# Turning softmax probabilities with a diagonal of reciprocals, in a two-block transformer kernel

## The chip, the cores and the metric

One NeuronCore of one Trainium2 chip. The metric is the device time of one execution in microseconds (us), the median of several executions. TensorE is called PE in the profile, its weight loads PEld, VectorE is DVE, ScalarE is ACT, GpSimd is POOL and the queue that issues the transfers is SP.

## The reference

Two blocks of two layers each, on one sequence of 256 tokens and 1024 features, in float32. Three of the stages are attention with a softmax, and these are all that the change touches:

```python
# "mla": 8 heads, query/key 128+64 wide, value 128
p = jax.nn.softmax(sc, axis=-1); o = jnp.einsum('bhqk,bkhd->bqhd', p, v)
# "even": 8 heads with a forget decay (fox), then 8 heads over a shared latent (dsa) with a top-64 choice
p = jax.nn.softmax(s, axis=-1);  ... p = jax.nn.softmax(logits, axis=-1)
# "moba": 16 heads of 64, causal (the 256 tokens are one block of keys)
p = jax.nn.softmax(s_own, axis=-1)
```

Around them stand a conformer convolution, squared-ReLU and gated feed-forward layers, and normalizations. Their matrix products take most of the time.

## The kernel before

All activations lie with features on the partitions and the 256 tokens along the free axis. Weights stream from memory in units of 128 x 4096 float32 values. ACT makes the high float16 part of each half unit (`w_hi`, line 1358), DVE the low part (`w_lo`, line 1992), and a product of float32 quality is three float16 products (lines 618 to 620, also 629 to 631, 1236 to 1238, 1294 to 1296), each 128 x 128 weights against 256 columns. Every engine runs a list of instructions written out by hand, and semaphores join them. Each engine takes its own list strictly in order.

The softmax works with queries on the partitions. A head's scores are two spans beside each other, the first 128 queries against 128 keys and the second 128 queries against 256 keys: 384 columns (`SPAN`). The steps of a head `hd`, with the semaphores of the table `A` in brackets:

- PE multiplies queries and keys in float32 into PSUM (line 786 in "mla" and "even", line 1261 in "moba") [`scores`].
- DVE scales, masks and takes the row maximum (lines 2132 and 2569), then negates it into `peak[2:4]` (lines 2136 and 2572) [`peak`].
- ACT writes `probs = exp(score - max)` and the row sums into `peak[4:6]` (lines 1458 and 1845) [`exp`].
- DVE writes the reciprocals of the two sums into `peak[6:8]` (lines 2144 and 2579) [`inv`].
- POOL multiplies the rows of `probs` by them, in place, one instruction for each span (`divide`, line 1914, and `divide_pair`, line 1960) [`norm`].
- PE turns the three 128 x 128 blocks of `probs` into PSUM with `pe.transpose` against the constant `ident` (lines 797 and 1272) [`turn`]. In these instructions `probs` is the stationary operand and `ident` the moving one.
- ACT copies the turned block to `probsT` (lines 1467 and 1854) [`probsT`]. PE multiplies the values by it (lines 819, 820 and 1283) [`out`]. ACT and DVE split the output into two float16 parts (`x_hi` line 1481 and `x_lo` line 2147, `f_hi` line 1834 and `f_lo` line 2584) [`o_hi`, `o_lo`].

In "mla" and "even" the function `attention` runs on each engine, one step `i` for each head. In step `i` PE makes the scores of head `i`, turns head `i - 3` (`TURN_LAG`) and multiplies the values of head `i - 4` (`OUT_LAG`). In "mla" a slice of the following product `wo` runs between heads (line 629). In step `i` DVE reduces head `i`, inverts the sums of head `i - 1`, makes one `x_lo` and splits a quarter of a weight half (line 2116). The buffers are `probs` three deep, and `peak`, `scores` and `probsT` two deep.

In "moba" the heads go in eight pairs, woven into the projections of the following pair. PE's loop, and around it DVE's:

```python
for p in range(last_pair):              # PE
    pair_product(p + 1, 0, 0, DC // 2); swap_pair(p)
    pair_product(p + 1, 0, DC // 2, DC); pair_product(p + 1, 1, 0, DC // 2)
    score_pair(p)
    if p: turn_pair(p - 1)
    pair_product(p + 1, 1, DC // 2, DC)
    if p: out_pair(p - 1)
# DVE: invert_pair(p - 1), low_pair(p - 2), rope_pair(p), weight splits, reduce_pair(p)
```

`rope_pair` (lines 2556 and 2559) needs `swap_pair` of PE (line 1248) and POOL's `cosine` (line 1950), and `score_pair` needs `rope_pair`. After the loop PE begins the output product `outo` (`behind_pairs`, line 1294), first waiting for ACT to have evacuated the last projection (line 1814). ACT does that behind the exponentials of pair 6.

## Time and profile before

| | us |
|---|---|
| median of 3 runs | 1237.71 |
| lowest and highest of them | 1233.33, 1250.34 |
| the profiled execution | 1241.19 |
| its span, from first to last instruction | 1239.4 |

The page of the profile gives the busy time of each engine, the chain of work that ended last, and groups of instructions. Besides it, the trace can be asked for the instructions of one engine in order of time, for who waited for whom, and for the busy time of each engine in chosen stretches. The attention stages lie at about 359 to 400 us ("mla"), 671 to 734 us ("even") and 949 to 1036 us ("moba"). A float32 product appears as two instructions, each with its own weight load. A turning with `pe.transpose` appears as one.

### The profile page before, as it was taken

The numbers are of one execution on the slowest core, as the hardware profiler recorded it, in microseconds if no ns is written. First come the engines' busy times: TensorE is split into PE (matmuls) and PEld (weight loads), VectorE is DVE, ScalarE is ACT, GpSimd is POOL, SyncE is SP. The second block draws the span as 40 slices with busy tenths as digits, with TensorE's granted clock in tenths as the row PEclk, the third lists the DMA queues.
The fourth block names the chain that finished last, engine by engine and source line by source line (L and its number), as shares of the span: only waits on it lengthen the run. The fifth ranks groups of instructions, "written<-read, shape, count | busy, mean of one in ns | idle before, by whom it ended". The sixth has DMA issues, their size and how long they took to land.

```text
span 1239.4 us, 26482 instructions
## 1 busy us (share of the span) xinstructions
PE 1190.2 (96%) x10692; PEld 998.2 (81%) x10692; DVE 831.9 (67%) x1352; ACT 661.3 (53%) x1046; POOL 128.2 (10%) x160
## 2 busy tenths in 40 slices
PE   8999999999989999999989999999999987999997
PEld 6778888888757888888875668888887766888886
DVE  6766786655954886655695447877666654887764
ACT  6564566433655566433453656665446654765432
POOL 0000100000122100000211421000123531000000
PEclk9998999999998999999999999999999999999998
DMA  7650365555341355555361033654565332555451
GB/s 318 244 200 24 108 233 203 204 203 203 104 169 68 136 204 203 204 203 203 115 226 69 8 129 136 216 199 163 182 233 196 136 137 77 201 205 197 149 196 63
DMA packets 17932, 206.58 MB, mean 167 GB/s; under 512 B 1984, under 2 KB 3392, under 8 KB 5056
## 3 DMA queue, kind: packets, MB, share of 16 engines
q1 hardware_dynamic: 17856, 205.52, 45.7%
q8 instruction: 54, 0.88, 0.3%
q14 instruction: 22, 0.18, 0.0%
HBM read 204.46 MB, written 1.05 MB: 166 GB/s over the span
## 4 chain that ended last, share of the span: by engine, by line
PE 82%; DVE 10%; ACT 4%; DMA 2%; issue 2%; POOL 0%; SPq 0%; DVEq 0%; ACTq 0%
PE ps L618 20%; PE ps L620 20%; PE ps L619 20%; PE ps L786 4%; DVE w_lo L1992 3%; DMA staged<-weights 2%; PE ps L884 2%; ACT w_hi L1358 1%; DVE stat L2006 1%; PE ps L819 1%; PE ps L629 1%; PE ps L1236 1%; PE ps L734 1%; PE ps L631 1%; PE ps L1237 1%
## 5 line engine op out<-in xcount | busy, mean ns | idle before, releaser
L1358 ACT ACTIVATE w_hi<-staged 128x2048 f16<-128x2048 f32 (+3 forms) x191 | 337.3, 1783 | 247.7 <-PE ps L620 212.9
L618 PE MATMUL ps<-f_hi,w_hi 128*128 128x256 f16 x1628 | 444.9, 273 | 8.3 <-DVE h L2086 7.1
L619 PE MATMUL ps<-f_lo,w_hi 128*128 128x256 f16 x1628 | 444.9, 273 | 0.0
L620 PE MATMUL ps<-f_hi,w_lo 128*128 128x256 f16 x1628 | 444.9, 273 | 0.0
L1992 DVE SCALAR_TENSOR_TENSOR w_lo<-staged,w_hi 128x2048 f16<-128x2048 f32 (+3 forms) x191 | 407.4, 2148 | 40.0 <-ACT w_hi L1358 39.8
L618 PE MATMUL ps<-x_hi,w_hi 128*128 128x256 f16 x880 | 240.1, 273 | 0.7 <-DVE tmp L2282 0.6
L620 PE MATMUL ps<-x_hi,w_lo 128*128 128x256 f16 x880 | 239.9, 273 | 0.0
L619 PE MATMUL ps<-x_lo,w_hi 128*128 128x256 f16 x880 | 239.9, 273 | 0.0
L618 PEld LDWEIGHTS ps<-f_hi,w_hi 128*128 128x128 f16 x1628 | 159.7, 98 | 28.5 <-DVE h L2086 7.4
L619 PEld LDWEIGHTS ps<-f_lo,w_hi 128*128 128x128 f16 x1628 | 159.7, 98 | 19.5
L620 PEld LDWEIGHTS ps<-f_hi,w_lo 128*128 128x128 f16 x1628 | 159.7, 98 | 18.9
L618 PEld LDWEIGHTS ps<-x_hi,w_hi 128*128 128x128 f16 x880 | 86.1, 98 | 17.6 <-issue 5.0
L619 PEld LDWEIGHTS ps<-x_lo,w_hi 128*128 128x128 f16 x880 | 86.1, 98 | 11.0
L620 PEld LDWEIGHTS ps<-x_hi,w_lo 128*128 128x128 f16 x880 | 86.1, 98 | 10.0
L1922 POOL TENSOR_TENSOR h<-h,m 128x256 f32<-128x256 f32 x28 | 23.9, 882 | 503.6 <-DVE m L2039 503.6
L2308 DVE TENSOR_SCALAR m<-ps 128x256 f32 (+1 forms) x16 | 6.8, 424 | 63.4 <-PE ps L620 54.4
L1761 ACT ACTIVATE tmp<-pad,vec 128x256 f32<-128x256 f32 x44 | 26.4, 599 | 42.1 <-DVE pad L2473 37.9
L2282 DVE SCALAR_TENSOR_TENSOR tmp<-ps,stat 128x256 f32<-128x256 f32 x64 | 26.8, 419 | 26.2 <-PE ps L620 26.1
L2473 DVE TENSOR_TENSOR pad<-ps,stat 128x256 f32<-128x256 f32 x44 | 18.6, 423 | 31.6 <-PE ps L620 31.6
L1458 ACT ACTIVATE probs<-scores,peak 128x128 f32<-128x128 f32 (+1 forms) x48 | 21.4, 446 | 28.9 <-DVE peak L2136 28.9
L1592 ACT ACTIVATE tmp<-tmp 128x256 f32<-128x256 f32 x64 | 26.2, 409 | 17.4 <-DVE tmp L2282 17.4
L1914 POOL TENSOR_TENSOR probs<-probs,peak 128x128 f32<-128x128 f32 (+1 forms) x48 | 28.5, 615 | 64.9 <-DVE peak L2144 64.9
(312 smaller groups left out, 1680.8 us busy)
## 6 DMA issues: line engine op xcount, KB each, us to landing
staged<-weights SPq DMA_DIRECT2D x82, 2048.0 KB, 8.0
staged<-weights SPq DMA_DIRECT2D x16, 1408.0 KB, 6.1
xn<-bands SPq DMA_DIRECT2D x3, 512.0 KB, 9.6
m<-bands SPq DMA_DIRECT2D x3, 512.0 KB, 8.4
cst<-constants SPq DMA_DIRECT2D x1, 1029.0 KB, 10.5
h<-x_turned SPq DMA_DIRECT2D x2, 512.0 KB, 5.0
staged<-weights SPq DMA_DIRECT2D x2, 512.0 KB, 7.0
staged<-weights SPq DMA_DIRECT2D x1, 1024.0 KB, 9.2
```

The lines of the kernel that those rows point to most:

```text
L618: pe.matmul(out, wh, xh[:, c, :], start=(c == 0), stop=False)
L619: pe.matmul(out, wh, xl[:, c, :], start=False, stop=False)
L620: last = pe.matmul(out, wl, xh[:, c, :], start=False, stop=(c == kc - 1))
L786: last = pe.matmul(o[:, P * t:P * t + P * (t + 1)], a, b, start=(n == 0), stop=(n == len(terms) - 1))
L884: last = pe.matmul(ps[BAND * g:BAND * g + BAND, 3, 0:T], banded[w][:, (j * TAP_SET + g) * TAP_STEPS + step, :], shifted[:, j % 2, x, g, TA ...
L1358: act.activation(w_hi[:, s, o:o + n], staged[:, s, o:o + n], ACT.Copy, scale=SW).then_inc(hi_split, 1)
L1592: act.activation(tmp[:, 2 + n % 2:3 + n % 2, :], r, ACT.Square)
L1761: act.activation(tmp[:, j, :], pad[:, j, 0:T], ACT.Identity, bias=vec[:, bass.ds(i * 4 + (VCOL[f"b_cv_{layer}"] + n), 1)], scale=vec[:, ba ...
L1914: last = pool.tensor_tensor(probs[:, hd % 3, sl], probs[:, hd % 3, sl], peak[:, hd % 2, 6 + t:7 + t].to_broadcast([P, P * (t + 1)]), ALU.mult)
L1922: pool.tensor_tensor(h[:, c, :], h[:, c, :], m[:, c, :], ALU.add).then_inc(h_ready[ready], 1)
L1992: dve.scalar_tensor_tensor(w_lo[:, s, o:o + n], staged[:, s, o:o + n], SW, w_hi[:, s, o:o + n], ALU.mult, ALU.subtract).then_inc(lo_split, 1)
L2282: dve.scalar_tensor_tensor(tmp[:, n % 2, :], ps[:, n % RING, 0:T], 0.0, LATE_SCALE, ALU.max, ALU.mult).then_inc(drained[one], 1)
```

## The change

GpSimd's `divide` and `divide_pair` are gone. After its reciprocal, VectorE waits for that reciprocal to be written, makes two 128 x 128 diagonals for the head (`ident` times the reciprocal of each row) in a new buffer `shares_diag`, and raises `norm` itself. TensorE turns with an ordinary float32 product: `probs` stays the stationary operand, the moving operand is the diagonal in place of `ident`, and so the turned block comes out scaled. VectorE's wait ahead of the reciprocal is now for the turning of the head (or pair) that used the buffer before, where it was for GpSimd's scaling.

```diff
+        shares_diag = sb("shares_diag", [P, 2, TT, P])
@@ tensor, attention
                         for n in range(3):
-                            last = pe.transpose(o[:, P * n:P * n + P], probs[:, hd % 3, P * n:P * n + P], k("ident"))
+                            last = pe.matmul(o[:, P * n:P * n + P], probs[:, hd % 3, P * n:P * n + P],
+                                             shares_diag[:, hd % 2, min(n, 1), :], start=True, stop=True)
@@ tensor, turn_pair
-                        last = pe.transpose(ps[:, 6 + r, P * n:P * n + P], probs[:, (2 * p + r) % 3, P * n:P * n + P], k("ident"))
+                        last = pe.matmul(ps[:, 6 + r, P * n:P * n + P], probs[:, (2 * p + r) % 3, P * n:P * n + P],
+                                         shares_diag[:, r, min(n, 1), :], start=True, stop=True)
@@ gpsimd
-            def divide(kind):
-                at = before(kind)
-                for hd in range(KINDS[kind]["heads"]):
-                    pool.wait_ge(A["inv"], at["inv"] + hd + 1)
-                    for t in range(TT):
-                        sl = slice(P * t, P * t + P * (t + 1))
-                        last = pool.tensor_tensor(probs[:, hd % 3, sl], probs[:, hd % 3, sl],
-                                                  peak[:, hd % 2, 6 + t:7 + t].to_broadcast([P, P * (t + 1)]), ALU.mult)
-                    last.then_inc(A["norm"], 1)
-            divide("mla")
-            divide("even")
-            def divide_pair(p):
-                ...
-                if p:
-                    divide_pair(p - 1)
-            divide_pair(last_pair)
@@ vector, attention
-                            dve.wait_ge(A["norm"], at["norm"] + hd - 1)
+                            dve.wait_ge(A["turn"], at["turn"] + hd - 1)
                         dve.reciprocal(peak[:, b, 6:8], peak[:, b, 4:6]).then_inc(A["inv"], 1)
+                        dve.wait_ge(A["inv"], at["inv"] + hd + 1)
+                        for t in range(TT):
+                            last = dve.tensor_scalar(shares_diag[:, b, t, :], k("ident"), peak[:, b, 6 + t:7 + t], None, ALU.mult)
+                        last.then_inc(A["norm"], 1)
@@ vector, invert_pair
-                    dve.wait_ge(A["norm"], heads["norm"] + p)
+                    dve.wait_ge(A["turn"], heads["turn"] + p)
                 dve.reciprocal(peak[:, :, 6:8], peak[:, :, 4:6]).then_inc(A["inv"], 1)
+                dve.wait_ge(A["inv"], heads["inv"] + p + 1)
+                for r in range(2):
+                    for t in range(TT):
+                        last = dve.tensor_scalar(shares_diag[:, r, t, :], k("ident"), peak[:, r, 6 + t:7 + t], None, ALU.mult)
+                last.then_inc(A["norm"], 1)
```

## Rows read from the trace of the kernel before

**Rows 1.** Page, part 1: busy us (share of the span) and instructions of each engine.

```profile
PE 1190.2 (96%) x10692; PEld 998.2 (81%) x10692; DVE 831.9 (67%) x1352; ACT 661.3 (53%) x1046; POOL 128.2 (10%) x160
```

**Rows 2.** Page, part 4: the chain that ended last, by engine.

```profile
PE 82%; DVE 10%; ACT 4%; DMA 2%; issue 2%; POOL 0%; SPq 0%; DVEq 0%; ACTq 0%
```

**Rows 3.** Busy us of each engine by stretch, then PEclk, DMA share, GB/s.

```profile
367.00:382.00 15.00, 14.28 (x38) 8.65 (x38) 2.82 (x19) 7.33 (x25) 3.88 (x8) 0.56 0.00 1
672.00:716.00 44.00, 42.52 (x203) 26.42 (x201) 18.59 (x92) 25.82 (x81) 16.46 (x26) 1.00 0.09 29
948.00:1014.60 66.60, 66.17 (x525) 48.82 (x522) 44.42 (x94) 39.83 (x84) 33.02 (x37) 1.00 0.38 132
1014.60:1018.00 3.40, 0.16 (x3) 0.14 (x2) 1.85 (x12) 2.37 (x11) 0.17 (x1) 0.89 0.93 390
1018.00:1036.00 18.00, 17.55 (x143) 14.06 (x143) 5.96 (x16) 5.57 (x13) 4.31 (x9) 0.93 0.39 142
```

**Rows 4.** Timeline of PE, a dsa head: start us, us, engine line op tiles.

```profile
700.27 0.49 PE L786 MATMUL ps<-kT,m 128*128 128x128 f32 x2
700.69 0.49 PE L786 MATMUL ps<-qT 64*128 64x128 f32 x2
...
702.36 0.55 PE L797 MATMUL ps<-cst,probs 128*128 128x128 f32 x3
702.84 0.65 PE L819 MATMUL ps<-probsT,f_lo 128*64 128x256 f32 x2
```

**Rows 5.** Timeline of PE, a pair of "moba".

```profile
966.57 0.88 PE L1272 MATMUL ps<-cst,probs 128*128 128x128 f32 x6
967.28 0.27 PE L1236 MATMUL ps<-x_hi,w_hi 128*128 128x256 f16 x1
```

**Rows 6.** Timeline of PE, line 696: two float32 products, broadcast column against `ident`.

```profile
130.43 0.61 PE L696 MATMUL ps<-cst,by_token 128*128 128x128 f32 x4
130.87 1.03 PE L734 MATMUL ps<-decay_k 128*128 128x256 f32 x4
```

**Rows 7.** Timeline of PE, "mla" at the low clock.

```profile
367.72 6.86 PE L786 MATMUL ps<-kT,qT 128*128 128x128 f32 x16 [2.06 <-ACT qT L1428]
...
374.51 0.90 PE L797 MATMUL ps<-cst,probs 128*128 128x128 f32 x3
375.20 3.66 PE L786 MATMUL ps<-kT,qT 128*128 128x128 f32 x8
```

**Rows 8.** Timeline of PE: its idle times behind a turning [idle before <-releaser].

```profile
393.60 0.67 PE L819 MATMUL ps<-probsT,f_lo 128*128 128x256 f32 x2 [1.28 <-DVE x_lo L2147]
...
716.96 0.67 PE L819 MATMUL ps<-probsT,ckvt 128*128 128x256 f32 x2 [0.95 <-DVE x_lo L2147]
...
726.24 0.67 PE L819 MATMUL ps<-probsT,ckvt 128*128 128x256 f32 x2 [0.50 <-ACT tmp L1475]
...
1017.85 0.37 PE L1294 MATMUL ps<-f_hi,w_hi 128*128 128x256 f16 x1 [3.24 <-issue]
```

**Rows 9.** Timeline of DVE, "even", the step in which head 9 is turned.

```profile
715.58 0.29 DVE L2132 CUSTOM_DVE_ANT_0 scores<-ps,sel 128x128 f32<-128x128 f32 x1 [1.51 <-PE ps L786]
...
716.33 0.17 DVE L2144 RECIPROCAL peak<-peak 128x2 f32<-128x2 f32 x1
716.41 0.40 DVE L2147 SCALAR_TENSOR_TENSOR x_lo<-ps,x_hi 128x256 f16<-128x256 f32 x1
```

**Rows 10.** Timeline of DVE, "moba": an undisturbed rope, then around the rope of pair 6.

```profile
1000.31 0.69 DVE L2559 TENSOR_TENSOR qT<-qT,tmp 128x512 f32<-128x512 f32 x1
...
1006.45 0.18 DVE L2579 RECIPROCAL peak<-peak 128x4 f32<-128x4 f32 x1 [1.75 <-ACT probs L1845]
1006.99 0.42 DVE L2584 SCALAR_TENSOR_TENSOR f_lo<-ps,f_hi 128x256 f16<-128x256 f32 x1 [0.36 <-ACT f_hi L1834]
1008.26 0.69 DVE L2556 TENSOR_TENSOR tmp<-ps,tmp 128x512 f32<-128x512 f32 x1 [0.84 <-PE ps L1248]
1008.98 0.91 DVE L2559 TENSOR_TENSOR kT<-kT,tmp 128x512 f32<-128x512 f32 x1
```

**Rows 11.** Timeline of DVE: a 128x128 and a 128x256 scaling by a column.

```profile
635.87 0.54 DVE L2418 TENSOR_SCALAR idx<-scores,gates 128x128 f32<-128x128 f32 x2
```

**Rows 12.** Timeline of POOL, "moba": a cosine and a scaling of a pair.

```profile
1006.77 0.73 POOL L1950 TENSOR_TENSOR kT<-kT,tmp 128x256 f32<-128x256 f32 x1 [2.98 <-ACT kT L1814]
1007.45 1.90 POOL L1960 TENSOR_TENSOR probs<-probs,peak 128x128 f32<-128x128 f32 x4
```

**Rows 13.** Line 797: its idle before, by releaser: us, times.

```profile
L797 PE MATMUL ps<-cst,probs x72: 272/273/473, 374.5 to 729.6; 128*128 128x128 f32 x72
its engine sat idle before it (us, times) until:
  issue: 6.1, 16
```

**Rows 14.** Page, part 5: GpSimd's scaling of single heads: busy, mean ns | idle before.

```profile
L1914 POOL TENSOR_TENSOR probs<-probs,peak 128x128 f32<-128x128 f32 (+1 forms) x48 | 28.5, 615 | 64.9 <-DVE peak L2144 64.9
```

More of the change, by code:

```diff
@@ L1951, in cosine @@
                     normed_rows, 1)
-            def divide_pair(p):
-                pool.wait_ge(A["inv"], heads["inv"] + p + 1)
-                for r in range(2):
-                    for t in range(TT):
-                        sl = slice(P * t, P * t + P * (t + 1))
-                        at = probs[:, (2 * p + r) % 3, sl]
-                        last = pool.tensor_tensor(at, at, peak[:, r, 6 + t:7 + t].to_broadcast([P, P * (t + 1)]), ALU.mult)
-                last.then_inc(A["norm"], 1)
             pool.wait_ge(tables, 2)
```

## The prediction

> **What bounds the kernel now.** I read the page first. TensorE is busy 96% of the span and holds 82% of the chain that ended last, GpSimd is busy 10% and holds none of it [rows 1, 2]. An average over the span says little about three attention stages, so next came the busy time by stretch. In "even" and in "moba" up to its end TensorE is busy 42.52 of 44 us and 66.17 of 66.6 us, at the full granted clock, while VectorE has more than a quarter of each stretch free [rows 3]. There every tenth that TensorE's list grows is a tenth of the end. The exceptions are four idle times that lie behind a turning [rows 8], and a part of "mla" at the low clock (0.56 granted on the mean over 15 us, so about 13.2 of the 15 at half speed) [rows 3].
>
> Then, who waits for the instruction that the change removes. The idle time ahead of the turning, 6.1 us in 16 places, ends on "issue", none of it on GpSimd's `probs` [rows 13]. This label belongs to the weight loads, which are not always back to back. No turning waits for a scaling: scores and turning are three steps apart, and the scaling of a pair takes 1.90 us [rows 12]. So removing GpSimd's 80 instructions takes nothing from the path.
>
> **The change part by part.**
>
> *GpSimd's scaling goes: 0.* What hides it now is the lag of three heads. No work waits behind it in its list that TensorE waits for either: each `cosine` that a pair needs stands ahead of the scaling of the pair before.
>
> *The turning becomes a product: the main term.* A turned block is one instruction today. A float32 product is two. The nearest row is line 696, float32, 128 x 128 stationary against 128 columns of `ident`, the same form as the new turning: its two products are four instructions that start within 0.44 us, 0.11 us each [rows 6]. Turned blocks go at about 0.11 us each as well: six of them and the switch to the next kind take 0.71 us [rows 5], three take 0.48 us [rows 4]. So a head gets three more instructions of 0.11 us, 0.33 us. The first of a group, whose load nothing covers, counts a little more: the second of a float32 product starts 0.49 - 0.27 = 0.22 us behind it, the second of a turning 0.55 - 0.27 - 0.11 = 0.17 us [rows 4], with 0.27 us for the last one's own duration. That adds 0.05. A head costs 0.38 us more, a pair 6 x 0.11 + 0.05 = 0.71 us.
>
> The bounds of this price: not under 0.33 us, since no row has a float32 product of 128 columns in less than two times 0.11 us. At most what line 786 shows, 0.42 us for a product of the same size (700.27 to 700.69) [rows 4]. There the second load is not hidden. I take the low end, because line 786 changes from 128 to 64 rows between products and the new turning, like line 696, doesn't.
>
> - "mla", 8 heads. Heads 0 and 1 are turned at the low clock (0.69 us from 374.51 to 375.20 for three blocks [rows 7]), so they pay double, 0.76 us. Heads 4 and 5 are turned ahead of 1.28 us of idle that ends on `x_lo` of VectorE, which hangs on the scores of head 7 and not on the turning [rows 8]: nothing. 2 x 0.76 + 4 x 0.38 = **3.0 us**.
> - "even", 16 heads: 16 x 0.38 = 6.1 us. Head 9 is turned ahead of 0.95 us of idle, and one idle time of 0.50 us near the end takes up what it can [rows 8]: 6.1 - 0.38 - 0.50 = **5.2 us**, before VectorE's part.
> - "moba", 8 pairs. Pair 5 is turned between the swap of pair 6 and the idle time of 3.24 us, whose end hangs on VectorE's rope, two weight splits and the reduction of pair 6, and then ACT's exponentials [rows 8, 10]: nothing. 7 x 0.71 = **5.0 us**.
>
> *VectorE's diagonals.* 80 new instructions of 128 x 128. The row of two scalings by a column, 128 and 256 wide, takes 0.54 us together [rows 11]. A head's two are at most that, a pair's four 1.08 us; below, 0.2 us each if only the width counts. I take the upper end. Then the wait for the reciprocal's own result, and the wait for the turning two heads back. A new turning of three blocks ends about 0.9 us after the scores, and VectorE reaches its reciprocal 0.75 us after it begins to reduce [rows 9], so that wait costs it some 0.15 us. What is queued behind: the `x_lo` of the step, a quarter split, and the next reduction. The reduction is covered, since VectorE has 1.51 us idle ahead of it [rows 9] against 0.7 us more work. The `x_lo` is covered everywhere but where TensorE waits for it. Head 9 is that place: its `x_lo` starts at 716.41 right behind the reciprocal [rows 9] and comes about 0.15 + 0.54 + 0.06 = **0.75 us** later. In "mla" the `x_lo` at the 1.28 us of idle waits for ACT, and hides the diagonals.
>
> In "moba" VectorE has 0.36 us of idle ahead of `low_pair` and 0.84 us ahead of the rope, 1.20 us together against 1.08 us [rows 10]. Without that cover the rope and the scores behind it would be late. It does hold, by little, so **0**. A rule of the Trainium skill speaks against this. The second SBUF port of VectorE is shared with GpSimd, and instructions that use two ports block each other (Advanced Engine Details and Errata, VectorE Performance Modes, Mode Summary). The trace has a sign of it: the rope's addition takes 0.91 us beside a scaling of GpSimd and 0.69 us where none runs [rows 10, 12]. By that rule the four diagonals would be stretched by the cosine of 0.73 us that runs at the same time, while the rope's addition would get its 0.22 us back, and the sum would be up to 0.4 us higher at pair 6 and unchanged elsewhere. The sum goes by the rows.
>
> **Sum**: 3.0 + 5.2 + 0.75 + 5.0 = 14.0 us. The profiled execution took 1241.2 us and would take 1255.2. It lies 3.5 us above the median of the runs shown, so against the median of 1237.7 I forecast **1252 us**, 1.1% slower. That is within the 2% (24.8 us) which I count as no change, about what a measurement of this kernel can tell.
>
> **The rivals.**
>
> *The loads are not hidden (ends on the other side, slower by over 2%).* Place: the six loads of a turning. Price: 0.42 us a block, as line 786 has it. A head goes from 0.48 to 1.26 us, +0.78, a pair from 0.71 to 2.52 us, +1.81. 24 x 0.78 + 8 x 1.81 = 33.2 us, plus 1.6 for two heads at the low clock, less the idle times that take up some (1.28, 0.50 and pair 5's 1.81): 31 us, so 1269 us. It decides from about 0.32 us a block on: 0.21 us more than today for 120 blocks is 25 us. For it: the two-instruction products of line 786 beside the turning. Against it: rows 6, the very form. 12%.
>
> *The clock stays up.* If TensorE worked at the full clock in "mla" where it has the low one now, 13.2 us of the stretch would take half, 6.6 us back, and the doubled price of two heads falls to the simple one, 0.8 us. The smaller stretch about 1018 us (0.89 over 3.4 us and 0.93 over 18 us, together 3.3 us at half speed [rows 3]) gives back 1.6 us, since the idle ahead of it shrinks from 3.24 to about 2.5 us. 14.0 - 9.0 = 5 us: 1243 us. Against it: the fall in "mla" follows an idle time of 2.06 us ahead of the first turning [rows 7], which no part of the change touches. 12%. The Trainium skill has a rule by which more would come of this: a turning in transpose mode doesn't count as activity for the clock gate (TensorE: Matmul & The Clock Gate, Part 4: PE-mode transpose), and an ordinary product would. By it the low stretch of "mla" would end sooner, for the part of the 6.6 us that is left when head 0 is turned at 374.5. The trace doesn't bear it out: in "even" the clock stays at 1.00 with a turning in every step [rows 3].
>
> *VectorE becomes the bound in "moba".* The cover of 1.20 us fails when the four diagonals run beside a cosine: 1.08 + 0.73 = 1.81 us, 0.6 us over, for 7 pairs 4.3 us, so 1256 us. Against it: the scores of a pair wait a further while for their place in TensorE's list. 10%.
>
> **How the numbers follow.** The forecast has 66%, the three rivals 12, 12 and 10%. The range is 1243 to 1264 us: the clock case at its lower end, the VectorE case inside, and it leaves out the case of unhidden loads and the tails. The three runs of before differ by 17 us, so a few us on either side are the measurement's own. Slower by over 2% is the first rival and a little, 13%. Faster by over 2% would need 25 us that no row offers, 1%. Within 2%: 86%.
>
> **What would show it.** TensorE's instructions grow by 120, to 10812, and nothing on GpSimd waits for `peak` any more. The groups at lines 797 and 1272 show 144 and 96 instructions, a head's six start within about 0.66 us, a pair's twelve within 1.3 us. GpSimd's busy time falls by some 44 us (28.5 in the 24 single heads, 8 x 1.90 = 15 in the pairs) [rows 12, 14], VectorE's grows by about 20 us. The idle time of 0.95 us at head 9 stays about as long, that of 3.24 us shrinks by 0.7 us, and VectorE's idle ahead of the rope nearly vanishes. The prediction is wrong if products in a group start 0.2 us apart, if TensorE waits for VectorE's rope or `norm` in "moba", or if the low clock in "mla" is gone.

## The result

| us, median | before | after |
| --- | --- | --- |
| first chip, 4 runs each | 1238.81 | 1260.41 |
| lowest, highest | 1233.33, 1250.34 | 1258.18, 1261.68 |
| the profiled execution, its span | 1241.19, 1239.4 | 1258.18, 1256.4 |

The ratio of after to before is 1.014, with a 95% interval from 1.009 to 1.020. The quotient of the two medians is 1.017. The kernel is slower, by less than 2%. The forecast was 1252 us in a range from 1243 to 1264. Ratios and intervals in this document leave out the runs that took over 1.5% longer than the fastest of their kernel, medians are of all runs.

The profile after. First the busy time of each engine and the chain that ended last, beside [rows 1, 2]:

```profile
PE 1208.2 (96%) x10812; PEld 1014.3 (81%) x10812; DVE 852.1 (68%) x1432; ACT 661.6 (53%) x1046; POOL 83.4 (7%) x80
...
PE 83%; DVE 9%; ACT 3%; DMA 3%; issue 1%; SPq 0%; POOL 0%; DVEq 0%; ACTq 0%
```

TensorE has 120 instructions more and 18.0 us more of busy time. The span is 17.0 us longer. GpSimd lost 44.8 us of busy time, and the end didn't move towards the start by anything for it: GpSimd held 0% of the chain, and still does. VectorE took on 20.2 us.

The timeline of TensorE around turnings: a head of "even", a pair of "moba" and the pair after it, and a head of "mla" at the low clock. They answer to [rows 4, 5, 7]. Columns are start us, us, engine line operation tiles.

```profile
710.58 0.94 PE L799 MATMUL ps<-shares_diag,probs 128*128 128x128 f32 x6
711.44 0.65 PE L822 MATMUL ps<-probsT,f_lo 128*64 128x256 f32 x2
...
978.98 1.60 PE L1275 MATMUL ps<-shares_diag,probs 128*128 128x128 f32 x12
980.42 0.27 PE L1239 MATMUL ps<-x_hi,w_hi 128*128 128x256 f16 x1
...
988.38 1.60 PE L1275 MATMUL ps<-shares_diag,probs 128*128 128x128 f32 x12
...
375.18 1.65 PE L799 MATMUL ps<-shares_diag,probs 128*128 128x128 f32 x6
376.62 0.63 PE L788 MATMUL ps<-kT,qT 128*128 128x128 f32 x2
```

A head's turning takes 0.86 us up to the next instruction, where it took 0.48. A pair's takes 1.44 us, where it took 0.71. At the low clock a head takes 1.44 us, where it took 0.69. So the three surcharges are 0.38, 0.73 and 0.75 us. Two pairs follow each other at 9.40 us (978.98 to 988.38). Before, the same two stood 8.68 us apart (966.57 to 975.25 by [rows 5] and the row of line 1272 behind it): the surcharge shows in the period, and nothing else in such a step of "moba" grew.

TensorE's idle times behind a turning, beside [rows 8]. The value in brackets is the idle time before the row and what ended it:

```profile
396.74 0.67 PE L822 MATMUL ps<-probsT,f_lo 128*128 128x256 f32 x2 [0.35 <-DVE x_lo L2129]
...
727.44 0.67 PE L822 MATMUL ps<-probsT,ckvt 128*128 128x256 f32 x2 [1.27 <-DVE x_lo L2129]
...
1032.96 0.27 PE L1298 MATMUL ps<-f_hi,w_hi 128*128 128x256 f16 x1 [2.29 <-issue]
```

They were 1.28, 0.95 and 3.24 us. The same three points also measure how far the kernel is behind: 396.74 against 393.60 is 3.1 us at the end of "mla", 727.44 against 716.96 is 10.5 us late in "even", 1032.96 against 1017.85 is 15.1 us near the end of "moba".

The busy time of each engine by stretch, in the columns of [rows 3], for the low clock in "mla", a stretch ahead of "even", and most of "even" and "moba":

```profile
368.30:385.30 17.00, 17.00 (x46) 10.66 (x44) 4.34 (x25) 6.27 (x20) 0.00 (x0) 0.50 0.00 1
651.60:655.00 3.40, 3.40 (x18) 2.35 (x17) 3.37 (x5) 0.00 (x0) 0.00 (x0) 0.50 0.63 265
684.00:727.00 43.00, 40.69 (x201) 27.09 (x198) 24.16 (x112) 26.55 (x84) 0.72 (x1) 1.00 0.12 44
965.00:1030.00 65.00, 64.96 (x510) 49.10 (x512) 46.12 (x106) 36.01 (x73) 17.99 (x12) 1.00 0.36 130
```

"even" and "moba" are bound by TensorE at the full clock, as before. "mla" has the low one for 17 us, and there is a stretch of 3.4 us at the low clock ahead of "even" which the trace of before doesn't have.

**Where the 17.0 us are**, by the distance between the same instructions of the two traces:

| part | us | forecast |
| --- | --- | --- |
| ahead of the first turning | 0.7 | 0 |
| "mla" | 3.15 | 3.0 |
| between "mla" and "even" | 2.3 | 0 |
| "even" | 5.55 | 5.95 |
| "moba" | 5.17 | 5.0 |
| behind it | 0.15 | 0 |

The three stages that turn give 13.9 us, where the working gave 14.0. That they agree so closely is partly luck, as the section on the prediction shows. The other 3 us lie where nothing was changed, and the medians show still more, 21.6 us. That is what was left to explain.

### The profile page after: what moved, and what is told of

It is laid out like the page before. It is cut to its first block, busy times and chain, and to the rows that moved or that the text cites. A ratio compares the mean times of both kernels' runs of the same rounds, so it can differ in the third digit from the quotient of the medians.

```text
span 1256.4 us, 26722 instructions
## 1 busy us (share of the span) xinstructions
PE 1208.2 (96%) x10812; PEld 1014.3 (81%) x10812; DVE 852.1 (68%) x1432; ACT 661.6 (53%) x1046; POOL 83.4 (7%) x80
## 3 DMA queue, kind: packets, MB, share of 16 engines
HBM read 204.46 MB, written 1.05 MB: 164 GB/s over the span
## 4 chain that ended last, share of the span: by engine, by line
PE 83%; DVE 9%; ACT 3%; DMA 3%; issue 1%; SPq 0%; POOL 0%; DVEq 0%; ACTq 0%
PE ps L620 20%; PE ps L621 19%; PE ps L622 19%; PE ps L788 4%; DVE w_lo L1970 3%; DMA staged<-weights 2%; PE ps L887 2%; PE ps L799 2%; ACT w_hi L1362 1%; PE ps L1239 1%; PE ps L822 1%; PE ps L1240 1%; PE ps L1241 1%; DVE stat L1984 1%; PE ps L1275 1%
## 5 line engine op out<-in xcount | busy, mean ns | idle before, releaser
L2256 DVE SCALAR_TENSOR_TENSOR f_lo<-tmp,f_hi 128x256 f32 (+1 forms) x64 | 26.7, 418 | 14.1 <-ACT f_hi L1597 13.6
## 6 DMA issues: line engine op xcount, KB each, us to landing
cst<-constants SPq DMA_DIRECT2D x1, 1029.0 KB, 10.5
```

What stands on the lines that cost most here:

```text
L2256: dve.scalar_tensor_tensor(f_lo[:, at, :], f, SF, f_hi[:, at, :], ALU.mult, ALU.subtract).then_inc(f_lo_ready[layer], 1)
```

## The experiments

The main theory is that of the prediction: the whole loss is TensorE's second instruction for each turned block, the work taken from GpSimd is worth nothing, and VectorE's diagonals are hidden but at one head. The first rival says that VectorE's diagonals cost the time, as they stand ahead of `x_lo` and of the rope. The second says that the granted clock does: that the changed kernel, by its nature, spends another time at the low clock.

Each execution comes with its span and its mean granted clock. The clock has two levels here, full and half, 2.4 and 1.2 GHz, and so the time at the low one is 2 x span x (1 - clock). Over the executions of the kernel before on the chips of the experiments (21, 23 and 33 on the three), the spans lie on 1223.4 us + 0.41 x that time, with a standard deviation of 1.4 us and at most 3.8 us off. So each kernel gets two numbers: the mean time at the low clock, and the **steady part**, its span less 0.41 of that time. The 0.41 is fitted to the kernel before and taken over for the others.

| kernel | runs | median us | ratio to before, 95% | low clock, us | steady part, us |
| --- | --- | --- | --- | --- | --- |
| before (three chips) | 21, 23, 33 | 1243.84, 1243.87, 1244.62 | 1 | 41, 47, 45 | 1223.6, 1223.1, 1223.6 |
| after (first chip) | 4 | 1260.41 | 1.014 [1.009, 1.020] | 54 | 1236.4 |
| after, again | 10 | 1251.36 | 1.0089 [1.0054, 1.0125] | 37 | 1235.2 |
| product alone | 6 | 1257.14 | 1.0136 [1.0085, 1.0187] | 47 | 1235.2 |
| diagonals alone | 6 | 1256.35 | 1.0102 [1.0036, 1.0168] | 74 | 1223.0 |
| VectorE scales | 12 | 1246.94 | 1.0044 [1.0008, 1.0080] | 59 | 1222.9 |
| product twice | 6 | 1277.55 | 1.0263 [1.0205, 1.0321] | 34 | 1260.8 |
| after, `x_lo` first | 6 | 1254.93 | 1.0119 [1.0057, 1.0182] | 47 | 1235.2 |
| VectorE scales, `x_lo` first | 12 | 1243.74 | 1.0009 [0.9967, 1.0051] | 44 | 1223.7 |
| float16 turning | 12 | 1247.25 | 1.0002 [0.9964, 1.0040] | 61 | 1219.0 |
| before, one gap filled | 12 | 1238.49 | 0.9974 [0.9940, 1.0009] | 34 | 1223.1 |
| before, three gaps filled | 12 | 1236.11 | 0.9931 [0.9904, 0.9958] | 21 | 1225.2 |
| after, three gaps filled | 12 | 1247.93 | 1.0035 [1.0008, 1.0062] | 18 | 1238.6 |
| float16 turning, three gaps filled | 10 | 1234.93 | 0.9920 [0.9895, 0.9946] | 31 | 1219.9 |

### The changed kernel again, on another chip

No edit.

> The changed kernel once more. The traces of before and after differ by 13.9 us in the stretches that turn, and by 17.0 us in the span, while the medians differ by 21.6 us. Theory A (the second instruction of each turning product is all of it, the rest is scatter of the runs and low clock elsewhere): 14 to 17 us over before. Rival B (there is a further steady loss that one pair of traces doesn't show): 20 to 23 us over before again.

1251.36 us, a ratio of 1.0089. The loss is 7.5 us by the medians here, against 21.6 us on the first chip. Neither theory had it: 14 to 17 and 20 to 23 us were expected. The steady part is 11.6 us above that of before on the same chip, and was 1236.4 against 1235.2 us for the changed kernel itself. What differs is the time at the low clock: 54 us and 37 us for one and the same program. The busy time by stretch shows it in "mla", here 13.7 us in the columns of [rows 3], in which before and the first trace of after have about half the clock:

```profile
367.50:381.20 13.70, 13.70 (x68) 9.18 (x68) 6.80 (x35) 8.36 (x27) 0.00 (x0) 1.00 0.01 1
```

68 instructions in 13.7 us at the full clock, where the first trace of after had 46 in 17 us. The idle time ahead of "mla" is the same in both, 2.05 and 2.06 us.

### The product alone

GpSimd scales as before, VectorE makes no diagonals. Only the form of the turning changes.

```diff
-last = pe.transpose(o[:, P * n:P * n + P], probs[:, hd % 3, P * n:P * n + P], k("ident"))
+last = pe.matmul(o[:, P * n:P * n + P], probs[:, hd % 3, P * n:P * n + P], k("ident"), start=True, stop=True)
```

The pair's turning has the same edit.

> The kernel before, with the turning as an ordinary float32 product against the constant identity. GpSimd still scales, VectorE makes no diagonals. Theory A (TensorE's instructions are the loss): 13.2 us over before (3.0 in mla, 5.2 in even, 5.0 in moba), a head's group of six instructions 0.38 us longer, a pair's 0.73. Rival C (VectorE's diagonals and its wait for the turning carry a good part): at most 8 us over before.

A steady part of 1235.2 us, the same as that of the changed kernel and 11.6 us above before. The groups are those of after too, here a head of "even", head 9 with the product behind it, and two pairs on TensorE's timeline:

```profile
705.31 0.94 PE L797 MATMUL ps<-cst,probs 128*128 128x128 f32 x6
706.18 0.65 PE L819 MATMUL ps<-probsT,f_lo 128*64 128x256 f32 x2
...
716.22 0.94 PE L797 MATMUL ps<-cst,probs 128*128 128x128 f32 x6
717.72 0.67 PE L819 MATMUL ps<-probsT,ckvt 128*128 128x256 f32 x2 [0.56 <-DVE x_lo L2147]
...
969.25 1.60 PE L1272 MATMUL ps<-cst,probs 128*128 128x128 f32 x12
970.70 0.27 PE L1236 MATMUL ps<-x_hi,w_hi 128*128 128x256 f16 x1
...
978.66 1.60 PE L1272 MATMUL ps<-cst,probs 128*128 128x128 f32 x12
```

0.87 us for a head, 1.45 us for a pair, 9.41 us from pair to pair. With GpSimd's scaling back in place and VectorE's work gone, the whole steady loss is still there. So it is TensorE's, and neither GpSimd's nor VectorE's part of the change moves it by more than such a comparison can tell, about half a us. The rows can tell more: at head 9 the next product starts 1.50 us behind the turning here, just as before (715.47 to 716.96), so the longer turning hides in the idle time, which fell from 0.95 to 0.56 us.

### The diagonals alone

VectorE makes the diagonals and GpSimd is free, but the turning stays `pe.transpose` with `ident`. The division of the softmax is left out.

```diff
-last = pe.matmul(o[:, P * n:P * n + P], probs[:, hd % 3, P * n:P * n + P],
-                 shares_diag[:, hd % 2, min(n, 1), :], start=True, stop=True)
+last = pe.transpose(o[:, P * n:P * n + P], probs[:, hd % 3, P * n:P * n + P], k("ident"))
```

> The changed kernel with the old turning by transpose, so VectorE makes the diagonals and raises the semaphore, and nothing reads them. The probabilities stay unscaled: the softmax division is left out. Theory A: 0.7 us over before, all of it in the wait for x_lo at head 9 (idle 0.95 us grows to 1.6), within the scatter. Rival C (VectorE is what costs): 6 us or more over before. If removing GpSimd's scaling gave something back, it would be under before.

The median, 12.5 us above before, taken alone would have spoken for the rival that blames VectorE. The steady part doesn't: 1223.0 us against 1223.6. All of the difference is time at the low clock, 74 us against 41 on this chip, and 0.41 x 33 = 13.5 us. The trace has the pairs at the period of before (967.16 to 975.84, 8.68 us), and a stretch in "even" at the low clock that neither before nor after shows in theirs. Busy time by stretch, in the columns of [rows 3]:

```profile
719.00:736.00 17.00, 16.69 (x44) 10.54 (x45) 5.47 (x24) 6.41 (x22) 0.00 (x0) 0.50 0.08 32
```

So the diagonals are hidden. That this kernel stayed at the low clock for longer is measured in its six runs, one of which is left out of the ratio. Why is not settled (below).

### VectorE scales the probabilities in place

No diagonals, no product: VectorE does what GpSimd did, 128 and 256 columns by a column, and the turning stays a transposition.

```diff
-last = dve.tensor_scalar(shares_diag[:, b, t, :], k("ident"), peak[:, b, 6 + t:7 + t], None, ALU.mult)
+at_t = probs[:, hd % 3, P * t:P * t + P * (t + 1)]
+last = dve.tensor_scalar(at_t, at_t, peak[:, b, 6 + t:7 + t], None, ALU.mult)
```

> GpSimd's scaling is gone, VectorE scales the probabilities in place with two instructions a head (128 and 256 wide, where the diagonals were 128 and 128), and the turning stays a transpose. The output is the whole one. Theory A: 1 us over before at most, 13 us under the changed kernel, though VectorE does slightly more than for the diagonals. Rival C: no better than the changed kernel.

A steady part of 1222.9 us. This frees GpSimd just as the change does, and costs TensorE nothing that the steady part shows. The ratio of 1.0044 again comes with more time at the low clock, 59 us.

### The product twice

Each product of the turning is issued twice, into the same place and with the same operands. It adds 120 products, 240 instructions.

```diff
+pe.matmul(o[:, P * n:P * n + P], probs[:, hd % 3, P * n:P * n + P], shares_diag[:, hd % 2, min(n, 1), :],
+          start=True, stop=True)
 last = pe.matmul(o[:, P * n:P * n + P], probs[:, hd % 3, P * n:P * n + P],
```

> The changed kernel with every turning product run twice into the same place. Theory A (each further instruction costs TensorE 0.11 us wherever it has no idle time): a head 0.67 us more, a pair 1.34, together 22 to 25 us over the changed kernel, span times granted clock about 1256 (changed kernel 1232, before 1220). Rival (TensorE's list has slack that took part of the change up): under 15 us.

The steady part is 25.6 us above that of the changed kernel, 0.107 us for each added instruction. TensorE's timeline of one pair, which has twelve products of two instructions each. Here are the first four:

```profile
982.62 0.49 PE L1277 MATMUL ps<-shares_diag,probs 128*128 128x128 f32 x2
982.95 0.39 PE L1279 MATMUL ps<-shares_diag,probs 128*128 128x128 f32 x2
983.17 0.39 PE L1277 MATMUL ps<-shares_diag,probs 128*128 128x128 f32 x2
983.39 0.39 PE L1279 MATMUL ps<-shares_diag,probs 128*128 128x128 f32 x2
```

The starts are 0.22 us apart (0.33 for the first), so an instruction with its own weight load costs 0.11 us when another stands ahead of it. The price of line 696 [rows 6] holds in the attention stages, and the end moves by nearly all of TensorE's added time.

### `x_lo` ahead of the diagonals

Does the wait at head 9 cost anything? In VectorE's step the scaling to `x_lo` moves ahead of the reciprocal and the diagonals.

```diff
+for c, b, hd in ended(kind, i - LOW_LAG[kind]):
+    ...
 hd = i - 1
 if 0 <= hd < H:
     ...
-for c, b, hd in ended(kind, i - LOW_LAG[kind]):
-    ...
```

> The changed kernel with VectorE's x_lo ahead of the reciprocal and the diagonals in each step of mla and even. Theory A: the idle time at head 9 falls from 1.27 us to about 0.5, 0.7 us less in span times granted clock, nothing else moves. Rival (the order on VectorE matters elsewhere too): over 2 us either way.

TensorE's idle times that end on `x_lo`, in the timeline of this kernel, "mla" and then head 9:

```profile
388.31 0.67 PE L822 MATMUL ps<-probsT,f_lo 128*128 128x256 f32 x2 [1.00 <-DVE x_lo L2117]
...
718.25 0.67 PE L822 MATMUL ps<-probsT,ckvt 128*128 128x256 f32 x2 [0.49 <-DVE x_lo L2117]
```

The idle time at head 9 goes from 1.27 to 0.49 us, as it should if the diagonals delayed `x_lo`. But one in "mla" is 1.00 us, where the second trace of after has 0.35 us. From the turning to the next product it is 0.77 us less at head 9 (2.20 to 1.43 us) and 0.65 us more at that place of "mla" (1.19 to 1.84). The steady part stays at 1235.2 us, where 0.7 us less was expected. The term at head 9 is real, and this order pays for it in "mla".

The same order in the kernel in which VectorE scales:

> VectorE scales the probabilities in place, the turning is a transpose, and x_lo goes ahead of the reciprocal. Theory D (with transposes an idle time of TensorE in even is what brings the low clock there, and it costs 4 to 10 us): idle at head 9 back at 0.9 us or less, granted clock 0.98 or more as before, and 1 us under before. Rival (the low clock comes with any idle time, whatever is at head 9, since the one ahead of the first turning at 678 us stays at 1.48 us): granted clock 0.967 to 0.982 as without the new order.

1243.74 us, ratio 1.0009, a steady part of 1223.7 us. Its time at the low clock is that of before, 44 us, and its granted clocks run from 0.973 to 0.990 with a median of 0.982. That decides neither way between the two expectations. Theory D isn't borne out by the trace, which has a low stretch in "even" again, at about 677 to 687 us, long before head 9.

### Float16 for the probabilities and the diagonals

Both buffers become float16, so that the product is one instruction again. It rounds the probabilities and the reciprocals. The outputs differ from the float32 ones by 2% and not in the fourth digit, as the expectation has it, so this is a probe and no kernel to keep.

```diff
-probs = sb("probs", [P, 3, SPAN])
+probs = sb("probs", [P, 3, SPAN], F16)
-shares_diag = sb("shares_diag", [P, 2, TT, P])
+shares_diag = sb("shares_diag", [P, 2, TT, P], F16)
```

> The changed kernel with the probabilities and the diagonals in float16, so that a turned block is one float16 instruction in place of two float32 ones. Theory A (the price is the two float32 instructions of a block): the whole 12 us come back, a group of three takes about 0.35 us or less, span less 0.41 times the us at low clock between 1217 and 1224 (before 1223.7, changed 1235.7). Rival C (VectorE and the new waits): it stays above 1230. Rounding to float16 changes the values in the fourth digit.

TensorE's timeline, a head of "even" and two pairs:

```profile
705.48 0.34 PE L799 MATMUL ps<-shares_diag,probs 128*128 128x128 f16 x3
705.75 0.65 PE L822 MATMUL ps<-probsT,f_lo 128*64 128x256 f32 x2
...
968.63 0.51 PE L1275 MATMUL ps<-shares_diag,probs 128*128 128x128 f16 x6
968.98 0.27 PE L1239 MATMUL ps<-x_hi,w_hi 128*128 128x256 f16 x1
...
976.94 0.51 PE L1275 MATMUL ps<-shares_diag,probs 128*128 128x128 f16 x6
```

A head takes 0.27 us and a pair 0.35 us, and the pairs follow at 8.31 us, 0.37 less than before. The steady part is 1219.0 us, 16 to 17 below the changed kernel and 4.6 below before. All other parts of the change are in this kernel. Its median is no better than that of before, since it spent 61 us at the low clock.

### Filled gaps: the clock held still

The long low stretches that the traces have in "mla" and "even" begin behind idle times of TensorE, the one in "mla" behind 2.06 us [rows 7]. The same idle time is followed by the full clock in other traces, as in the second one of after. The kernel has `keep_warm(n)`, products whose result nobody reads, for such places. Here 4 more stand ahead of head 2 of "mla" in the kernel before:

```diff
+keep_warm(4, 7)
 pe.wait_ge(drained["uq"], 12)
 attention("mla", 2, behind="wo")
```

> The kernel before, with eight idle matmuls (four float32 products whose output nobody reads) in TensorE's idle time of 2.06 us ahead of head 2 in mla. Theory D (the idle time brings the low clock of 13.7 us at 368.7 in the trace of before): the stretch is at the full clock, granted clock 0.989 or more in nearly all executions, median 5 to 7 us under before. Rival (the sparse float32 products behind it bring it): granted clock 0.981 as often as before, no gain.

1238.49 us, a ratio of 0.9974, whose interval reaches 1.0009. The mean time at the low clock is 34 us against 47 on this chip. The steady part stays. The gain of 5.4 us by the medians is as large as expected, but not clear of noise.

Then three places: ahead of head 2 of "mla", ahead of head 2 of "even" and, in the second layer, ahead of the gated MLP.

```diff
+keep_warm(3, 7)
 pe.wait_ge(normed_rows, 9)
@@ glu_mlp
+if layer:
+    keep_warm(13, 3)
 pe.wait_ge(h_ready[("oute", "outo")[layer]], (DC - RING + 1, DC - 1)[layer])
```

> The kernel before with idle products in three idle times of TensorE: 4 ahead of head 2 in mla, 3 ahead of head 2 in even, 13 ahead of the last up projection, where it waits 7.14 us. Theory D (each low stretch follows an idle time): at most 23 us at low clock (start, and the last wait), median 8 to 10 us under before, span less 0.41 times low still 1223 to 1224. Rival (sparse products behind them bring it anyway): as with the first of the three alone, 34 us at low clock on the mean.

> The changed kernel with the same three fillings. Theory A: 12 to 13 us over the filled kernel before, and now with little scatter, since both have the same low stretches. Rival B (the change itself adds low clock): 15 us or more over it.

> The float16 turning with the three fillings. Theory A and D together: 8 to 14 us under before, under the filled kernel before by 0 to 6 us.

Before goes to 1236.11 us, 0.7% faster than it was, the fastest of the kernels that compute all that the reference does. The changed kernel with the same edit takes 1247.93 us. Busy time by stretch, of before with three filled gaps and then of the changed kernel with them, "mla" and the MLP behind "moba":

```profile
360.00:400.00 40.00, 38.30 (x236) 28.43 (x235) 19.87 (x71) 23.26 (x62) 8.30 (x16) 1.00 0.19 61
1040.00:1080.00 40.00, 38.30 (x322) 33.54 (x321) 31.99 (x42) 27.22 (x36) 4.53 (x7) 1.00 0.44 159
```

```profile
360.00:400.00 40.00, 39.23 (x243) 29.78 (x244) 22.21 (x84) 22.34 (x61) 0.00 (x0) 1.00 0.15 53
1040.00:1080.00 40.00, 38.31 (x322) 33.27 (x321) 23.01 (x31) 23.11 (x32) 5.20 (x7) 1.00 0.31 112
```

In all four the clock is full. With it nearly the same in both (21 and 18 us low, granted clock 0.991 and 0.992 by the medians), the twelve runs of each lie within 9 and 4 us, and their medians are **11.8 us** apart. The steady parts are 13.4 us apart. This is the cleanest measurement of the change. It hardly leans on the fit for the clock, as 3 us less at the low clock are worth 1.4 us. The float16 turning with the same three fillings takes 1234.93 us, 13.0 us under the changed kernel, though it has 31 us at the low clock against 18. The steady parts are 18.7 us apart. Both come from the float16 turning and what goes with it, since ACT and VectorE now write float16 too.

## Why the prediction was right, and where it was not

*GpSimd's scaling is worth nothing.* Right. The product alone, with the scaling back, has the same steady part as the changed kernel, and VectorE's scaling in GpSimd's place has that of before. GpSimd's busy time fell by 44.8 us, where 44 was announced.

*A product costs one more instruction of 0.11 us, with the load hidden.* Right, and this carried the forecast. 0.38, 0.73 and 0.75 us were measured for a head, a pair and a head at the low clock, where 0.38, 0.71 and 0.76 were written. The two-instruction products of line 786, at 0.42 us for one, are no measure for a group that changes nothing between its products. Doubling the products added 0.107 us an instruction. The 120 added instructions are there, and a group is over in 0.86 and 1.44 us, up to the next instruction, as the announced starts within 0.66 and 1.3 us ask for. The rival with unhidden loads falls: at the full clock no turning has its products 0.42 us apart.

*What the idle times take up.* Nearly right. At the end of "mla" the idle time went from 1.28 to 0.35 us: it took up 0.93, and two heads cost 0.76. Why it is more isn't settled, but the product alone has the same 0.35 us. In "moba" the idle time went from 3.24 to 2.29, 0.95 us where 0.7 was announced. The product alone leaves 2.52 us there, the diagonals alone 3.02. So 0.72 is the turning's and the other 0.22 comes with GpSimd's absence, as much as the rope's addition got shorter (below). The short idle time near the end of "even" took up 0.7 us and not 0.50: the step in which it lies went from 2.45 to 2.11 us from turning to turning, with a turning that is 0.39 us longer.

*VectorE's diagonals at head 9: the term of 0.75 us.* Right in its parts, and nearly in its size. TensorE's timeline of after and VectorE's in that step, beside [rows 9]:

```profile
725.23 0.94 PE L799 MATMUL ps<-shares_diag,probs 128*128 128x128 f32 x6
...
726.02 0.17 DVE L2114 TENSOR_SCALAR peak<-peak 128x2 f32<-128x2 f32 x1
726.28 0.17 DVE L2122 RECIPROCAL peak<-peak 128x2 f32<-128x2 f32 x1
726.48 0.48 DVE L2125 TENSOR_SCALAR shares_diag<-cst,peak 128x128 f32<-128x128 f32 x2
726.87 0.42 DVE L2129 SCALAR_TENSOR_TENSOR x_lo<-ps,x_hi 128x256 f16<-128x256 f32 x1
```

The row ahead of the reciprocal in before, and both rows in the float16 turning, whose turning is over in 0.34 us:

```profile
716.25 0.17 DVE L2136 TENSOR_SCALAR peak<-peak 128x2 f32<-128x2 f32 x1
```

```profile
718.89 0.17 DVE L2114 TENSOR_SCALAR peak<-peak 128x2 f32<-128x2 f32 x1
718.97 0.17 DVE L2122 RECIPROCAL peak<-peak 128x2 f32<-128x2 f32 x1
```

From the negation to the reciprocal it is 0.26 us in after and 0.08 us in both others. So VectorE waits 0.18 us for the turning of two heads back, where 0.15 had been written. Then `x_lo` starts 0.59 us behind the reciprocal, where it started 0.08 us behind it: 0.51 us more, by two diagonals at 0.20 us each from start to start and about 0.1 us of wait for the reciprocal. That had been 0.54 + 0.06 us, with the diagonals priced by a 128 and a 256 wide scaling [rows 11], where the lower bound of 0.2 us each was the true value. Together they make 0.69 us, and TensorE's next product starts 2.20 us behind the turning (725.23 to 727.44) where it started 1.50 us behind it before, and in the product alone. The diagonals alone, whose turning is short, have 2.02 us. So the turning itself costs nothing at this place, and the 0.70 us are VectorE's. One sign contradicted this sum: the idle time was to stay about as long, while 0.95 - 0.38 + 0.75 makes 1.32 us, and it grew to 1.27.

*"mla": 3.15 us against 3.0.* The near agreement is luck in part. The low stretch lasts 17 us in this trace of after and 13.7 in before, by which the step from head 1 to head 2 grew by 1.14 us and not by 0.75. The 0.2 us that the idle time took up beyond the sum stand against it. Between the two kernels with filled gaps, at the full clock on either side, "mla" costs 2.0 us, where six heads at the simple price make 2.3. The doubled price of two heads belongs to the execution and not to the change.

*"even" as a whole: 5.55 us against 5.95.* The price of a head in it was taken from one row of 0.48 us [rows 4]. Not all are alike. TensorE's timeline of before has heads at 0.42 us from the turning to the next instruction:

```profile
695.70 0.49 PE L797 MATMUL ps<-cst,probs 128*128 128x128 f32 x3
696.12 0.65 PE L819 MATMUL ps<-probsT,f_lo 128*64 128x256 f32 x2
```

and that of after has them at 0.76 us:

```profile
699.64 0.83 PE L799 MATMUL ps<-shares_diag,probs 128*128 128x128 f32 x6
700.40 0.65 PE L822 MATMUL ps<-probsT,f_lo 128*64 128x256 f32 x2
```

That is 0.34 us for such a head in place of 0.38. Five heads of "even" have this length, which accounts for 0.2 of the 0.4 us. The idle time near the end accounts for the other 0.2.

*"moba": 5.17 us against 5.0.* Here too two things cancel. The idle time took up 0.22 us more than the turning of a pair costs, and in the step behind it TensorE had some 0.3 us more at the low clock. In before 0.7 us of the low stretch about 1018 us lie in the idle time (0.89 granted over its 3.4 us [rows 3]), in after all of it falls on work (1.00 granted ahead of 1032.96).

*VectorE's cover in "moba": 0.* Right for the time. Here VectorE's timeline at pair 6, beside [rows 10]:

```profile
1021.78 0.18 DVE L2561 RECIPROCAL peak<-peak 128x4 f32<-128x4 f32 x1 [2.48 <-ACT probs L1849]
1022.00 1.35 DVE L2565 TENSOR_SCALAR shares_diag<-cst,peak 128x128 f32<-128x128 f32 x4
1023.26 0.41 DVE L2571 SCALAR_TENSOR_TENSOR f_lo<-ps,f_hi 128x256 f16<-128x256 f32 x1
1023.60 0.68 DVE L2538 TENSOR_TENSOR tmp<-ps,tmp 128x512 f32<-128x512 f32 x1
1024.31 0.69 DVE L2541 TENSOR_TENSOR kT<-kT,tmp 128x512 f32<-128x512 f32 x1
```

And GpSimd's at the same time:

```profile
1022.10 0.77 POOL L1941 TENSOR_TENSOR kT<-kT,tmp 128x256 f32<-128x256 f32 x1 [3.71 <-ACT kT L1818]
```

The four diagonals take 1.35 us beside a cosine of GpSimd, 1.26 up to the next instruction, where four undisturbed ones would take about 0.8 (0.20 each, as at head 9). One of them lasts 0.758 us by line 2565's longest, against a median of 0.278. The rope's addition is back from 0.91 to 0.69 us. VectorE's idle ahead of the rope is gone, as announced, and TensorE still doesn't wait for the rope: the period of the pairs is 9.40 us, all of it explained. No turning in "moba" waits for the diagonals either; near the end of "even" two weight loads are marked with 0.4 us of wait for them, but their steps are no longer than the turning explains (1.70 to 2.09 us). The rival that VectorE becomes the bound had the stretching right and the end wrong. The Trainium skill's rule on the shared SBUF port (Advanced Engine Details and Errata, VectorE Performance Modes, Mode Summary) agrees with this row in its direction, about 0.45 us for the four. The sum didn't grow by it, since TensorE's idle time behind pair 5 became 0.22 us shorter than its longer turning alone makes it.

*The clock.* Here my working was weakest, though the range held. I treated the low stretches of one execution as the kernel's own, and put "the clock stays up" as a mechanism of the changed kernel, with 12%, and the absence of the low clock in "mla" as what would prove me wrong. It is absent in the second trace of after, for reasons that aren't the change's. The runs show a scatter between executions of one program. "mla" has the full clock in the second trace of after, in the product alone and in the version with `x_lo` first, and the low one in the first trace of after, in the product twice, in before and in the diagonals alone. The kernel before was granted from 0.967 to 0.992 over its runs. At 0.41 us for each us at the low clock, that is why its times spread over 17 us on the first chip and over 24 on the second of the others (1232.97 to 1257.11). The first chip's gap of 21.6 us is then made of some 12 us that the change costs and the rest, some 9 us, of the low clock: four executions of after with 54 us of it, and a before whose median, at 1238.81, lies 5 us under that of each later chip. The split rests on the fit, and for before on that chip only the profiled execution has its clock on record, 0.982. That 1260 us lay inside the range, 8 us above the forecast, and 1251 us on the next chip right beside it, was then also a matter of which executions were caught. What doesn't rest on it is the pair with filled gaps, 11.8 us apart. The stretch of 3.4 us ahead of "even", with 1.69 us of idle before it in place of 1.05, is part of the same scatter as far as the traces show; what lengthens that idle time stays open.

*Where the sum stands.* The terms made 14.0 us, and the steady cost is 11.6 to 13.4 by the runs. The turning stages of the two traces gave 13.9, of which about 1.4 us are the low clock's: 0.75 by two heads at the doubled price, 0.4 by the longer low stretch in "mla" and 0.3 in "moba". The mechanism was right, but that the two sums agree to 0.1 us is luck.

*What stays open.* Which executions, and which kernels, get more of the low clock. The Trainium skill has the rule that a turning in transpose mode doesn't count as activity for the clock gate (TensorE: Matmul & The Clock Gate, Part 4: PE-mode transpose). The traces lean its way. Of the six kernels in float32 that turn by transposition, four have a low stretch in "even" (both with a free GpSimd, at 684 to 705 and 719 to 736 us in their traces, VectorE's scaling with `x_lo` first, and before with one gap filled), and none of the six traces in which the turning is a float32 product has one there. Here are two of them, in the columns of [rows 3], before with one gap filled and then the product twice:

```profile
676.00:696.40 20.40, 20.40 (x53) 11.92 (x53) 5.61 (x31) 8.12 (x27) 5.18 (x9) 0.50 0.00 0
```

```profile
672.00:734.00 62.00, 60.52 (x358) 43.56 (x356) 27.86 (x126) 28.27 (x88) 2.90 (x4) 1.00 0.08 27
```

Against it: the float16 turning is an ordinary product as well and has 61 us low, with 0.85 granted over 700 to 745 us, and even with its gaps filled a stretch of 3.4 us in "even"; the first chip's four executions of after have 54 us, more than before; and the low clock in "mla" comes and goes under either form. One trace a kernel doesn't settle it. By the rule the product would give back some of its price in some executions. A gain that the measurement can tell is not among the results: at the same time low, the product costs 11.6 to 13.4 us.

## What to carry to other kernels

Where TensorE is the bound, a float32 product in place of a float32 transposition costs a second instruction (0.11 us a block here), and work taken from an engine that holds none of the chain pays nothing for it; if GpSimd has to be freed, let VectorE do the scaling, in its own free time (1222.9 us steady here, where before has 1223.6). Before a loss or a gain of 1% is put down to an edit, look at the granted clock of every run and compare at equal clock. The nearest row of the same form, at whatever line, was worth more than a row of the same size with other shapes around it.

## What was unexpected of the hardware

- The same program was granted from 0.967 to 0.992 of the full clock, and its span followed at 0.41 us for each us at the low level. Half of that time would be lost if TensorE set the end throughout; the rest is hidden in its idle times or by the other engines. That last reading is argued, not measured.
- Work that computes nothing made the kernel faster: 40 instructions of filling ahead of three waits of TensorE brought 8.5 us by the medians, with a mean time at the low clock of 21 instead of 45 us. 0.41 x 24 is 9.8 us, less 1.6 us by which the steady part grew.
- VectorE's 128 x 128 float32 scaling by a column started every 0.20 us when two stood together and lasted up to 0.758 us beside a GpSimd operation of 0.77 us.
